# Spreading a norm's row over the partitions: one f32 product per 512 columns becomes two fp32r products of its halves

## The chip, the core and the metric

The kernel runs on one core of a Trainium2 chip. The metric is the device time of one execution in microseconds. Five engines matter: TensorE (PE in the profile; PEld is its weight load), VectorE (DVE), ScalarE (ACT), GpSimd (POOL) and SyncE (SP), which only issues loads and stores. They run side by side and wait for each other by semaphores.

## What is computed

One layer of a decoder step for a prompt of 512 tokens and 32 further tokens (8 sequences of 4). Cut to what matters here:

```
h = rmsnorm(x, g_mix_pre)            # x / sqrt(mean(x*x) + eps) * g, D = 1024
proj = h @ w_in                      # q, k, v, conv input, gelu input, gates
merged = sigmoid(ga) * (attention(q, k, v) @ w_pa) + sigmoid(gr) * (rglru(conv) * gelu(gb) @ w_pr)
x = x + rmsnorm(merged @ w_out, g_mix_post)
x = x + rmsnorm((silu(f @ wg) * (f @ wu)) @ w_down, g_ffn_post)     # f = rmsnorm(x, g_ffn_pre)
```

The change touches the first line: the row `g_mix_pre` (`norm_mix_pre`, 1024 numbers) has to stand in all 128 partitions, as x lies with its tokens on the partitions.

## The kernel before

All arithmetic is in f32 quality. TensorE's fast format for four-byte numbers is fp32r, which keeps fewer bits, so every large product is made of three: each operand is split into a high half (a copy into fp32r) and a low half (the number minus its high half, in fp32r again), and hi*hi, hi*lo and lo*hi are summed in PSUM (`steps`, line 1082; `head_pass`, line 1288). ScalarE makes the high halves of the weights (`hi`, line 1662), VectorE the low ones (`lo`, line 2248); the first low half is GpSimd's (line 946).

The prologue, up to about 20 us, brings x into place. SyncE loads x's token tiles (`x_tok`, four of 128 tokens and one of 32) and the first weights (`w_raw`). ScalarE squares and sums each tile (`x_rms`, line 1684) and takes the root (line 1687). VectorE inverts it (`x_inv`, line 2266) and scales the tile by it and by `g_row` (`x_scale`, line 2271). TensorE transposes the scaled tile (`x_T`, line 1106), ScalarE copies the result from PSUM to `xin_hi` (line 1696), VectorE subtracts to `xin_lo` (`x_lo`, line 2283). Then the first products can run (`head_pass`).

`g_row` comes about like this. VectorE zeroes partitions 0 to 126 of `g_one` (line 2237), and a load puts the norm's row in partition 127 (line 1672). `ones` is a 128x128 tile of ones. TensorE multiplies `ones` with `g_one` in f32, 512 columns at a time (`g_rows`, line 1116), so each partition of the result gets the sum over the partitions, which is the row. VectorE copies each half out of PSUM (`g_copy`, line 2261). Ahead of this, TensorE runs seven transposes of `ident` as fillers (`turn`, line 1113), and more of them between the transposes of x. Behind `g_rows`, TensorE makes the table of position biases (lines 1126 and 1127), which reuses a PSUM bank of the row and so waits for the first copy (`norm_step`), and for the loads of the table (`rel_in`). Behind the first products stand small transposes of parameters (lines 1299 and 1301), which wait for all the loads that GpSimd issues in the beginning (`par_in`).

Each engine works off its own list in the order in which it is written, and a wait holds up all that stands behind it. `norm_step` counts VectorE's steps of the norm; `consts_v` counts its constants; `g_in` is the load of the row. VectorE's order before is copy of g's first half, inverse of tile 0, scaling of its first half, copy of g's second half, scaling of the second half, then tile 1.

Of the kernel before, what the change touches and what calls it, by code (L numbers as in the profile page):

```python
# [23 lines left out]
F32 = mybir.dt.float32  # L24
F32R = mybir.dt.float32r
I32 = mybir.dt.int32
ALU = mybir.AluOpType
ACT = mybir.ActivationFunctionType
AP = bass.AP

P = 128
D = 1024
KD = D // P
# [3 lines left out]
T = SEQ + TS  # L37
# [74 lines left out]
X_ORDER = (0, 1, 2, 3, TT)  # L112
# [18 lines left out]
def program(nc, x_prompt, x_sample, cache_k, cache_v, page_table, state_conv, state_h,  # L131
# [11 lines left out]
    at = [-(-nc.sbuf_base // 64) * 64]  # L143

    def put(name, shape, dt=F32, where=None):
        size = 4 * int(np.prod(shape[1:]))
        size = -(-size // 32) * 32
        if where is None:
            offset, at[0] = at[0], at[0] + size
        else:  # L150
            offset, where[0] = where[0], where[0] + size
        assert offset + size <= nc.sbuf_usable_end, (name, offset + size)
        return nc.alloc_sbuf_tensor_at(name, shape, dt, offset=offset)
# [3 lines left out]
    w_raw, w_hi, w_lo = ring  # L157
    xin_at = at[0]
    xin_hi = put("xin_hi", [P, KD, T], F32R)
    xin_lo = put("xin_lo", [P, KD, T], F32R)  # L160
    ident = put("ident", [P, P])
    ones = put("ones", [P, P])
# [58 lines left out]
    x_sq = put("x_sq", [P, D], where=w)  # L221
    g_row = put("g_row", [P, D], where=w)
    g_one = put("g_one", [P, D], where=w)
    ssum = put("ssum", [P, 8], where=w)
    rstd_x = put("rstd_x", [P, 8], where=w)
    prow = put("prow", [56, P], where=w)
# [157 lines left out]
    with ExitStack() as ctx:  # L384
        def sem(name):
            return ctx.enter_context(nc.semaphore(name))

        ps = ctx.enter_context(nc.psum_tensor("ps", [P, 8, 512], F32))
# [12 lines left out]
        g_in = sem("g_in")  # L401
        g_spread = sem("g_spread")
# [4 lines left out]
        consts_v = sem("consts_v")  # L407
        sq_sum = sem("sq_sum")
        std_x = sem("std_x")
        norm_step = sem("norm_step")  # L410
# [160 lines left out]
        def x_fill(dst, tt, hf, f):  # L571

            if tt < TT:
                return (dst[:, 4 * hf:4 * hf + 4, tt * P:(tt + 1) * P],
                        ps[:, 4 + f % 4, :].rearrange("p (k c) -> p k c", c=P))
            return dst[:, :, SEQ:T], ps[:, 3, 0:KD * TS].rearrange("p (k c) -> p k c", c=TS)
# [495 lines left out]
        def _(e):  # L1072
# [37 lines left out]
            def turn(n):  # L1110

                for _ in range(n):
                    e.transpose(ps[:, 0, 0:P], ident[:, :], ident[:, :])

            def g_rows(hf):
                e.matmul(ps[:, 1 + hf, :], ones[:, :], g_one[:, 512 * hf:512 * hf + 512], start=True, stop=True  # L1116
                         ).then_inc(g_spread, 1)

            turn(7)
            e.wait_ge(consts_v, 6)  # L1120
            e.wait_ge(g_in, 16)
            g_rows(0)
            g_rows(1)
            e.wait_ge(norm_step, 1)
            e.wait_ge(rel_in, 32)
            e.matmul(ps[:, 3, 0:512], rel33[:, :], bktab[:, 0:512], start=True, stop=True)
            e.matmul(ps[:, 1, 0:RELW - 512], rel33[:, :], bktab[:, 512:RELW], start=True,
                     stop=True).then_inc(small_T, 1)
# [528 lines left out]
        def _(e):  # L1657
# [18 lines left out]
            e.dma_start(rel33[0:NB, 0:HEADS], rel_bias).then_inc(rel_in, 16)  # L1676
            e.wait_ge(consts_v, 5)
            e.activation(ycol[:, 0:1], eps_col[:, :], ACT.Sqrt)

            def x_rms(tt):  # L1680

                rows = P if tt < TT else TS
                e.wait_ge(x_in[tt], 16)
                e.activation(x_sq[0:rows, :], x_tok[0:rows, tt, :], ACT.Square,
                             accum_out=ssum[0:rows, tt:tt + 1]).then_inc(sq_sum, 1)
                e.wait_ge(sq_sum, X_ORDER.index(tt) + 1)
                e.activation(rstd_x[0:rows, tt:tt + 1], ssum[0:rows, tt:tt + 1], ACT.Sqrt,
                             bias=eps_col[0:rows, :], scale=1.0 / D).then_inc(std_x, 1)
# [539 lines left out]
        def _(e):  # L2228
# [30 lines left out]
            def g_copy(hf):  # L2259
                e.wait_ge(g_spread, hf + 1)  # L2260
                e.tensor_copy(g_row[:, 512 * hf:512 * hf + 512], ps[:, 1 + hf, :]).then_inc(norm_step, 1)

            def x_inv(tt):
                rows = slice(0, P if tt < TT else TS)
                e.wait_ge(std_x, X_ORDER.index(tt) + 1)
                e.reciprocal(rstd_x[rows, tt:tt + 1], rstd_x[rows, tt:tt + 1]).then_inc(norm_step, 1)

            def x_scale(tt, step, c0=0, c1=D):
                rows = slice(0, P if tt < TT else TS)
                e.wait_ge(norm_step, step)  # L2270
                e.scalar_tensor_tensor(x_tok[rows, tt, c0:c1], x_tok[rows, tt, c0:c1], rstd_x[rows, tt:tt + 1],
                                       g_row[rows, c0:c1], ALU.mult, ALU.mult).then_inc(xs_done, 1)

            def x_norm(tt):
                x_inv(tt)
                x_scale(tt, X_ORDER.index(tt) + 3)

            def x_lo(tt):
                for hf in range(2 if tt < TT else 1):
                    f = X_HALF[tt] + hf  # L2280
                    e.wait_ge(xt_hi, f + 1)
                    dst, src = x_fill(xin_lo, tt, hf, f)
                    e.tensor_tensor(dst, src, x_fill(xin_hi, tt, hf, f)[0].bitcast(F32), ALU.subtract).then_inc(xt_lo, 1)

            g_copy(0)
            x_inv(0)
            x_scale(0, 2, 0, 512)
            g_copy(1)
            x_scale(0, 3, 512, D)
            x_inv(1)  # L2290
            x_scale(1, 4, 0, 512)
            x_scale(1, 4, 512, D)
            x_lo(0)
            x_lo(1)
            x_norm(2)
            e.wait_ge(small_T, 3)
            e.tensor_copy(prm[:, :], ps[:, 2, 0:56]).then_inc(small_c, 1)
            e.tensor_copy(stT[:, :, :], ps[:, 2, 64:64 + P].rearrange("p (f r) -> p f r", f=PAIRS)).then_inc(small_c, 1)
            x_norm(3)
            e.wait_ge(lo_done, 3)  # L2300
            lo(1, 1)
            x_norm(TT)
            x_lo(2)
            x_lo(3)
# [500 lines left out]
            def y_square(m, s):  # L2805
                e.wait_ge(y_free, m + 3)
                if m > 1:
                    e.wait_ge(y_moved, min(m, KD - 3) * 192)
                e.transpose(yz[s][:, :], yg[s][:, :]).then_inc(y_turned, 1)  # L2809
                e.wait_ge(ysq_used, m + 1)  # L2810
                e.tensor_tensor(yacc[:, :], yacc[:, :], ysq[:, :], ALU.add).then_inc(ysq_used, 1)
# [13 lines left out]
            op_sums(0)  # L2825
            op_low(0, 5)
            e.memset(yacc[:, :], 0.0).then_inc(consts_v, 1)
            e.wait_ge(consts_v, 7)
            y_square(0, 0)
            op_low(0, 6)  # L2830
            hs_low(2, 3)
# [75 lines left out]
```

## Time and profile before

| | us |
|---|---|
| median of 3 runs | 761.62 |
| lowest and highest | 760.98, 761.72 |
| the profiled execution | 761.57 |
| its span, first to last instruction | 759.7 |
| TensorE busy in the span | 751.6 (99%) |
| VectorE, ScalarE, GpSimd busy | 519.8, 376.5, 116.4 |

All times in the profile are microseconds from the start of the span. A row of the timeline merges neighbouring instructions of one kind (x4 is four of them): its first number is the start of the first, the second the time from there to the end of the last. Matmuls are pipelined, so the time from one start to the next is what each costs, and the duration of one record is longer than that. A product in f32 has two records for 512 columns.

### The profile page before, as it was taken

The page shows a single profiled execution, that of the slowest core. Times are in us where ns is not written, and L with a number is a line of the kernel's source. Part 1 is how long each engine was busy: PE and PEld are TensorE (multiplying, and loading weights), DVE is VectorE, ACT ScalarE, POOL GpSimd, SP SyncE. Part 2 cuts the span into 40 slices and gives each one's busy share as a digit, 9 for nine tenths or more (in the row PEclk, how much of TensorE's full clock was granted, in tenths as well). Part 3 has the DMA queues.
Part 4 walks back from the last instruction along what each step waited for, and adds up shares of the span by engine and source line. Part 5 has one row for each costly group of instructions (what it writes and reads, how often), then busy time and mean ns, then how long its engine had stood idle before and what let it go on. Part 6 is the DMA issues. An engine that isn't in the chain of part 4 may idle for free.

```text
span 759.7 us, 16105 instructions
## 1 busy us (share of the span) xinstructions
PE 751.6 (99%) x5903; PEld 713.0 (94%) x5903; DVE 519.8 (68%) x823; ACT 376.5 (50%) x670; POOL 116.4 (15%) x228
## 2 busy tenths in 40 slices
PE   9999999999999999999999999999999999999996
PEld 6998899898898999997899999999999999999996
DVE  7547737656675574775469887787777899764644
ACT  7334625534733642344466555455554568454442
POOL 6502112020120110003000000000000000453650
PEclk9999999999999999999999999999999999999998
DMA  9645555545543325517461333223332212424274
GB/s 265 164 112 118 151 118 135 149 113 109 153 115 97 95 65 171 167 56 212 147 190 34 112 110 110 85 81 110 110 110 83 84 50 73 137 75 133 69 227 135
DMA packets 185065, 91.77 MB, mean 121 GB/s; under 512 B 52454, under 2 KB 177850, under 8 KB 185020
## 3 DMA queue, kind: packets, MB, share of 16 engines
q1 hardware_dynamic: 178958, 82.69, 39.8%
q0 software_dynamic: 4880, 8.13, 4.0%
q8 instruction: 28, 0.46, 0.3%
q10 hardware_dynamic: 1182, 0.35, 0.2%
q14 instruction: 17, 0.14, 0.1%
HBM read 82.37 MB, written 6.81 MB: 117 GB/s over the span
## 4 chain that ended last, share of the span: by engine, by line
PE 99%; ACT 0%; DVE 0%; DVEq 0%; issue 0%; POOL 0%; POOLq 0%
PE ps L1082 34%; PE ps L1470 28%; PE ps L1587 7%; PE ps L1365 6%; PE ps L1572 5%; PE ps L1534 4%; PE ps L1438 3%; PE ps L1288 2%; PE ps L1189 1%; PE ps L1203 1%; PE ps L1221 1%; PE ps L1263 1%; PE ps L1174 1%; PE ps L1234 1%; PE ps L1116 0%; PE ps L1373 0%
## 5 line engine op out<-in xcount | busy, mean ns | idle before, releaser
L1082 PE MATMUL ps<-xin_hi,w_hi 128*128 128x272 f32 x544 | 117.1, 296 | 0.0
L1082 PE MATMUL ps<-xin_hi,w_lo 128*128 128x272 f32 x544 | 112.6, 288 | 0.0
L1082 PE MATMUL ps<-xin_lo,w_hi 128*128 128x272 f32 x544 | 112.3, 288 | 0.0
L1082 PEld LDWEIGHTS ps<-xin_hi,w_hi 128*128 128x128 f32 x544 | 84.8, 189 | 8.1 <-issue 7.6
L2248 DVE TENSOR_TENSOR w_lo<-w_raw,w_hi 128x1024 fp32r<-128x1024 f32 (+1 forms) x46 | 55.9, 1216 | 47.6 <-ACT w_hi L1662 46.6
L1082 PEld LDWEIGHTS ps<-xin_lo,w_hi 128*128 128x128 f32 x544 | 85.5, 189 | 0.0
L1082 PEld LDWEIGHTS ps<-xin_hi,w_lo 128*128 128x128 f32 x544 | 85.0, 189 | 0.0
L648 POOL DMA_DIRECT2D ytok<-yz x48 | 33.8, 710 | 307.9 <-DVE yz L2809 307.9
L1662 ACT ACTIVATE w_hi<-w_raw 128x1024 fp32r<-128x1024 f32 (+1 forms) x47 | 49.2, 1050 | 47.9 <-PE ps L1082 44.0
L1470 PE MATMUL ps<-xq_lo,b_hi 128*128 128x272 f32 x160 | 46.7, 292 | 0.0
L1470 PE MATMUL ps<-xq_hi,a_lo 128*128 128x272 f32 x160 | 46.4, 290 | 0.0
L1470 PE MATMUL ps<-xq_lo,a_hi 128*128 128x272 f32 x160 | 46.2, 289 | 0.0
L1470 PE MATMUL ps<-xq_hi,b_hi 128*128 128x272 f32 x160 | 46.2, 289 | 0.0
L1470 PE MATMUL ps<-xq_hi,b_lo 128*128 128x272 f32 x160 | 46.1, 288 | 0.0
L1470 PE MATMUL ps<-xq_hi,a_hi 128*128 128x272 f32 x160 | 46.1, 288 | 0.0
L1470 PE MATMUL ps<-xq_hi,c_hi 128*128 128x272 f32 x160 | 46.1, 288 | 0.0
L1470 PE MATMUL ps<-xq_hi,c_lo 128*128 128x272 f32 x160 | 45.9, 287 | 0.0
L1470 PE MATMUL ps<-xq_lo,c_hi 128*128 128x272 f32 x160 | 45.9, 287 | 0.0
L1985 ACT ACTIVATE a_hi<-g_raw 128x1024 fp32r<-128x1024 f32 x20 | 21.2, 1062 | 21.1 <-PE ps L1470 17.9
L1470 PEld LDWEIGHTS ps<-xq_hi,b_hi 128*128 128x128 f32 x160 | 30.2, 189 | 0.0
L1470 PEld LDWEIGHTS ps<-xq_hi,b_lo 128*128 128x128 f32 x160 | 30.1, 188 | 0.0
L1470 PEld LDWEIGHTS ps<-xq_lo,a_hi 128*128 128x128 f32 x160 | 30.1, 188 | 0.0
(397 smaller groups left out, 2136.6 us busy)
## 6 DMA issues: line engine op xcount, KB each, us to landing
w_raw<-in_w_in_dram SPq DMA_DIRECT2D x68, 256.0 KB, 3.5
g_raw<-in_w_gate_up_dram SPq DMA_DIRECT2D x40, 256.0 KB, 3.8
u_raw<-in_w_gate_up_dram SPq DMA_DIRECT2D x20, 256.0 KB, 3.1
e_raw<-in_w_gate_up_dram SPq DMA_DIRECT2D x20, 256.0 KB, 4.3
raw_p<-in_w_down_dram SPq DMA_DIRECT2D x24, 192.0 KB, 2.5
kc<-in_cache_k_dram SPq DMA_DIRECT2D x64, 64.0 KB
vc<-in_cache_v_dram SPq DMA_DIRECT2D x64, 64.0 KB
raw<-in_w_down_dram SPq DMA_DIRECT2D x12, 320.0 KB, 3.2
```

Of the source, the lines that this page charges most:

```text
L648: e.dma_start(prompt[:, 2 * part:2 * part + 2, d, :], yz[s][rows, c0:c0 + 2 * P]).then_inc(moved, 16)
L1082: mm = e.matmul(ps[:, bank + h, 0:HT], wt[:, kw, :], xt[:, kx, h * HT:h * HT + HT], start=first and wt is wh and xt is xh, stop=last and ( ...
L1288: mm = e.matmul(ps[:, 2 * s + h, 0:cols.stop - cols.start], w[:, k, :], x[:, k, cols], start=first and k == 0, stop=last and k == KD - 1, ...
L1365: mm = e.matmul(ps[:, o_bank(tt) + c, :], xt[:, k, tt * P:tt * P + P], wt[:, c * NHALF:(c + 1) * NHALF], start=k == K_ORDER[0] and xt is x ...
L1438: mm = e.matmul(ps[:, 4 * m + 2 * c + h, 0:HT], wt[:, k, :], xt[:, x, k % KQ, :], start=k == 0 and wt is wh and xt is xq_hi, stop=k == KD ...
L1470: mm = e.matmul(ps[:, bank, 0:HT], wt[:, k0 + k, :], xt[:, x, k, :], start=first and k == 0 and wt is wh and xt is xq_hi, stop=last and k ...
L1534: mm = e.matmul(ps[:, D_BANK[odd] + h, 0:cols.stop - cols.start], wt[:, k, :], x, start=first and k == ks[0] and wt is wh and not lo_x, st ...
L1572: mm = e.matmul(ps[:, bank, 0:HT], wt[:, k, :], xt, start=first and k == 0 and wt is wh and xt is xh, stop=last and k == SK - 1 and wt is ...
L1587: mm = e.matmul(ps[:, banks[h], 0:HT], wt[:, k, :], x, start=firsts[h] and i == 0 and k == 0 and wt is wh and not lo_x, stop=lasts[h] and ...
L1662: e.activation((to or w_hi[s])[:, 0:k, :], w_raw[s][:, 0:k, :], ACT.Copy).then_inc(hi_done, count)
L1985: e.activation(a_hi[:, :, :], g_raw[s][:, :, :], ACT.Copy).then_inc(a_h, 1)
L2248: e.tensor_tensor(wl[:, 0:k, :], w_raw[s][:, 0:k, :], wh[:, 0:k, :].bitcast(F32), ALU.subtract).then_inc(lo_done, count)
```

## The change

It does four things. On VectorE, ahead of everything in the norm, `ones` is copied into an fp32r tile, g_one's first 512 columns are copied into `g_hi`, and the low halves of both parts are made by subtraction into `g_lo`. On ScalarE, after its first root and ahead of the first tile's squares, the other 512 columns are copied into `g_hi`. On TensorE, `g_rows` is two fp32r products (high half, then low half, into one PSUM group) and waits for the halves instead of the raw row; there are eleven filler transposes ahead of it instead of seven; and the bias table waits for a later count of the same semaphore, which is again that of the first copy out of PSUM. On VectorE both copies of `g_row` now come ahead of the inverse of tile 0, and both scalings of a tile wait for one count. The new tiles lie where `xin_lo` will be written later. The other hunks only renumber counts.

```diff
@@ tiles
+    xin_lo_at = at[0]
     xin_lo = put("xin_lo", [P, KD, T], F32R)
...
+    w_lo_ = [xin_lo_at]
+    g_hi = put("g_hi", [P, D], F32R, where=w_lo_)
+    g_lo = put("g_lo", [P, D], F32R, where=w_lo_)
+    ones_r = put("ones_r", [P, P], F32R, where=w_lo_)
@@ TensorE
             def g_rows(hf):
-                e.matmul(ps[:, 1 + hf, :], ones[:, :], g_one[:, 512 * hf:512 * hf + 512], start=True, stop=True
-                         ).then_inc(g_spread, 1)
-
-            turn(7)
-            e.wait_ge(consts_v, 6)
-            e.wait_ge(g_in, 16)
+                half = slice(512 * hf, 512 * hf + 512)
+                e.wait_ge(norm_step, 3 + hf)
+                e.matmul(ps[:, 1 + hf, :], ones_r[:, :], g_hi[:, half], start=True, stop=False)
+                e.matmul(ps[:, 1 + hf, :], ones_r[:, :], g_lo[:, half], start=False, stop=True).then_inc(g_spread, 1)
+
+            turn(11)
             g_rows(0)
             g_rows(1)
-            e.wait_ge(norm_step, 1)
+            e.wait_ge(norm_step, 5)
             e.wait_ge(rel_in, 32)
@@ ScalarE
             e.activation(ycol[:, 0:1], eps_col[:, :], ACT.Sqrt)
+            e.wait_ge(consts_v, 6)
+            e.wait_ge(g_in, 16)
+            e.activation(g_hi[:, 512:D], g_one[:, 512:D], ACT.Copy).then_inc(consts_v, 1)
@@ VectorE
+            e.wait_ge(consts_v, 6)
+            e.tensor_copy(ones_r[:, :], ones[:, :]).then_inc(norm_step, 1)
+            e.wait_ge(g_in, 16)
+            e.tensor_copy(g_hi[:, 0:512], g_one[:, 0:512]).then_inc(norm_step, 1)
+            e.wait_ge(norm_step, 2)
+            e.tensor_tensor(g_lo[:, 0:512], g_one[:, 0:512], g_hi[:, 0:512].bitcast(F32), ALU.subtract).then_inc(norm_step, 1)
+            e.wait_ge(consts_v, 7)
+            e.tensor_tensor(g_lo[:, 512:D], g_one[:, 512:D], g_hi[:, 512:D].bitcast(F32), ALU.subtract).then_inc(norm_step, 1)
             g_copy(0)
+            g_copy(1)
             x_inv(0)
-            x_scale(0, 2, 0, 512)
-            g_copy(1)
-            x_scale(0, 3, 512, D)
+            x_scale(0, 7, 0, 512)
+            x_scale(0, 7, 512, D)
             x_inv(1)
-            x_scale(1, 4, 0, 512)
-            x_scale(1, 4, 512, D)
+            x_scale(1, 8, 0, 512)
+            x_scale(1, 8, 512, D)
```

## Rows read from the trace of the kernel before

**Rows 1.** The page: its span, and the chain that ended last, by engine.
```profile
span 759.7 us, 16105 instructions
...
PE 99%; ACT 0%; DVE 0%; DVEq 0%; issue 0%; POOL 0%; POOLq 0%
```

**Rows 2.** Timeline of TensorE, 1.5 to 12 us: start, time, engine, line, operation, tiles.
```profile
1.53 1.76 PE L1113 MATMUL ps<-ident 128*128 128x128 f32 x7 [1.53 <-POOL ident L928]
...
2.87 0.42 PE L1113 MATMUL ps<-ident 128*128 128x128 f32 x1
...
3.21 3.78 PE L1116 MATMUL ps<-g_one,ones 128*128 128x512 f32 x4
6.86 1.55 PE L1126 MATMUL ps<-bktab,rel 128*128 128x512 f32 x2
...
8.47 0.60 PE L1106 MATMUL ps<-ident,x_tok 128*128 128x128 f32 x4
8.91 0.71 PE L1113 MATMUL ps<-ident 128*128 128x128 f32 x5
...
11.77 1.18 PE L1288 MATMUL ps<-xin_hi,w_hi 128*128 128x256 f32 x8 [0.19 <-ACT xin_hi L1696]
12.88 0.27 PE L1299 MATMUL ps<-ident,prow 56*128 56x56 f32 x1
```

**Rows 3.** Stretch 0 to 13 us: its length, busy times, granted clock, DMA.
```profile
0.00:13.00 13.00, 11.28 (x51) 7.44 (x51) 8.77 (x19) 8.26 (x15) 9.82 (x23) 1.00 0.86 269
```

**Rows 4.** Timeline of VectorE, 2.2 to 14 us.
```profile
2.24 0.91 DVE L2237 MEMSET g_one<- 127x1024 f32 x1 [0.16 <-issue]
5.32 0.69 DVE L2261 COPY g_row<-ps 128x512 f32<-128x512 f32 x1 [2.17 <-PE ps L1116]
6.36 0.16 DVE L2266 RECIPROCAL rstd_x<-rstd_x 128x1 f32<-128x1 f32 x1 [0.35 <-ACT rstd_x L1687]
6.56 0.75 DVE L2271 SCALAR_TENSOR_TENSOR x_tok<-x_tok,rstd_x,g_row 128x512 f32<-128x512 f32 x1
7.22 0.68 DVE L2261 COPY g_row<-ps 128x512 f32<-128x512 f32 x1
7.94 0.75 DVE L2271 SCALAR_TENSOR_TENSOR x_tok<-x_tok,rstd_x,g_row 128x512 f32<-128x512 f32 x1
...
8.80 1.41 DVE L2271 SCALAR_TENSOR_TENSOR x_tok<-x_tok,rstd_x,g_row 128x512 f32<-128x512 f32 x2
```

**Rows 5.** Timeline of ScalarE, 2 to 16.6 us.
```profile
3.64 0.20 ACT L1678 ACTIVATE ycol<-eps_col 128x1 f32<-128x1 f32 x1
4.85 1.06 ACT L1684 ACTIVATE x_sq<-x_tok 128x1024 f32<-128x1024 f32 x1 [1.00 <-DMA x_tok<-in_x_prompt_dram]
...
9.11 0.60 ACT L1696 ACTIVATE xin_hi<-ps 128x512 fp32r<-128x512 f32 x1 [1.09 <-PE ps L1106]
9.60 1.05 ACT L1662 ACTIVATE w_hi<-w_raw 128x1024 fp32r<-128x1024 f32 x1
10.55 1.56 ACT L1696 ACTIVATE xin_hi<-ps 128x512 fp32r<-128x512 f32 x3
```

**Rows 6.** Last parameter load: its issue, its us to landing; TensorE's wait at 16.49.
```profile
6.84 0.50 POOL L937 DMA_DIRECT2D strow<-in_state_h_dram  x1
...
strow<-in_state_h_dram POOLq DMA_DIRECT2D x1, 16.0 KB, 5.9
...
16.49 0.30 PEld L1288 LDWEIGHTS ps<-xin_hi,w_hi 128*128 128x128 f32 x2 [0.23 <-ACT w_hi L1662]
```

**Rows 7.** Chain that ended last, 0 to 40 us: start, us, what.
```profile
13.51 2.11 PE ps L1288 x16
```

**Rows 8.** VectorE's groups by form: busy, mean ns of one, idle before.
```profile
L2458 DVE TENSOR_SCALAR aa<-dd 128x552 f32<-128x552 f32 x4 | 1.8, 450 | 0.1
L2261 DVE COPY g_row<-ps 128x512 f32<-128x512 f32 x2 | 1.4, 688 | 2.2 <-PE ps L1116 2.2
L2369 DVE TENSOR_SCALAR lgt<-lgt,rden 128x128 f32<-128x128 f32 x8 | 2.3, 287 | 0.3
L2234 DVE MEMSET ones<- 128x128 f32 x1 | 0.2, 165 | 0.1
L2283 DVE TENSOR_TENSOR xin_lo<-ps,xin_hi 128x512 fp32r<-128x512 f32 x6 | 3.7, 674 | 0.0
```

More of the change, by code:

```diff
@@ L223, in program @@
     g_one = put("g_one", [P, D], where=w)
+    w_lo_ = [xin_lo_at]
+    g_hi = put("g_hi", [P, D], F32R, where=w_lo_)
+    g_lo = put("g_lo", [P, D], F32R, where=w_lo_)
+    ones_r = put("ones_r", [P, P], F32R, where=w_lo_)
+    assert w_lo_[0] <= xin_lo_at + 4 * KD * T
     ssum = put("ssum", [P, 8], where=w)
@@ L2275, in x_norm @@
                 x_inv(tt)
-                x_scale(tt, X_ORDER.index(tt) + 3)
+                x_scale(tt, X_ORDER.index(tt) + 7)
             def x_lo(tt):
@@ L2827, in _ @@
             e.memset(yacc[:, :], 0.0).then_inc(consts_v, 1)
-            e.wait_ge(consts_v, 7)
+            e.wait_ge(consts_v, 8)
             y_square(0, 0)
```

## The prediction

> **What bounds the kernel now.** I read the page from the top. TensorE is busy nearly all of the 759.7 us span, and the chain of work that ended last is 99% TensorE [rows 1]. The reader is to see that a prologue edit can only matter by when it lets TensorE's unbroken row of products begin: a microsecond that TensorE gains or loses in the first 20 us is carried to the end, and a microsecond of any other engine is worth nothing until TensorE waits for it. The profiled execution took 761.57 us, 1.87 us more than its span; the median of the three runs shown is 761.62 us, so the two agree within 0.05 us. I make the sum against 761.57.
>
> Next I read the prologue on each engine in order of time. On TensorE: seven transposes of `ident` that keep it busy, then the two products that spread the norm's row (four records of 128x512, two to a product), then the bias table, then the first transposes of x at 8.47, with filler transposes between, then the first real product at 11.77 [rows 2]. Two readings of those rows matter.
>
> First, TensorE's clock. The granted clock reads 1.00 for the first 13 us [rows 3], but the spacing of equal records says otherwise: seven `ident` transposes need 1.76 us, with a last one of 0.42 us some 0.21 us from start to start, while five of them at 8.91 need 0.71 us, some 0.11 us each [rows 2]. The four records of 512 columns take 3.78 us and the two of the bias table 1.55 us. So the engine works at the lower level (1.2 GHz) until about 7.8 us, in the middle of the bias table, and at 2.4 GHz after it. It had been at work since 1.53 us, with gaps of about 0.1 us.
>
> Second, who holds TensorE. The products of the norm's row end about 6.8 and the bias table begins at 6.86, so until 8.47 the engine only works off its queue. On VectorE the copy of g's first half waits until 5.32 for its product, and x_tok's first half is scaled from 6.56 to 7.31 [rows 4], over 1.1 us before TensorE takes it up. So before the change it is TensorE, not VectorE, that sets the first transposes. After them ScalarE is late: it idles until 9.11, then runs without a gap the copy to xin_hi, the high half of the first weights (9.60, 1.05 us) and three more copies [rows 5]; the first product waits for one of these, 0.19 us by its row [rows 2]. The transposes of parameters come next, at 12.88. They need every load on GpSimd's list; the last of these is issued at 6.84 and lands 5.9 us later, at 12.74 [rows 6]. That is 0.14 us before its use, and it doesn't move with this change.
>
> **The change part by part.** *Removed:* the two f32 products, 3.78 us of TensorE at the lower clock [rows 2]. By the rows the first needs 2.11 us from its start at 3.21 to the copy at 5.32; two records at 0.85 us (the spacing of the four) are 1.71 of it, and 0.40 is weight load, drain and hand-over.
>
> *Added on TensorE:* four fp32r products of 512 columns. The trace has none of these at the lower clock. Sixteen of 256 columns take 2.11 us at the higher one [rows 7], 0.13 each, so 512 columns at half the clock are 0.53; the floor is half an f32 record, 0.43. I take 0.45 a product: 0.9 a half instead of 1.71. Four more filler transposes (0.85 us) run from 3.0 to 3.9, while the engine would be waiting anyway: free.
>
> *Added on VectorE ahead of the products*, after its memset of g_one that ends 3.15 [rows 4]: a 128x128 copy, between the memset's 0.17 and a TENSOR_SCALAR's 0.29, I take 0.20; the high half of 512 columns, between 0.45 (one source, SBUF to SBUF, 552 columns) and 0.69 (the copy out of PSUM), I take 0.45, as the nearer shape; the low half, 0.68, from the TENSOR_TENSOR of 512 columns into fp32r [rows 8]. With 0.1 for the semaphore increments that stand before them and 0.05 at each of three hand-overs this is 3.15 + 0.1 + 0.20 + 0.45 + 0.68 + 0.15 = 4.73. TensorE begins the products there instead of at 3.21: **1.5 us later**. The second low half (0.68) runs on VectorE until 5.4, under the first pair of products.
>
> The Trainium skill ("VectorE: DVE Perf Modes", perf-mode tier table) says that a single-source fp32 op whose operands lie in SBUF takes two elements a cycle and one that reads PSUM only one. Its cost table would price the high half at 0.33 us, and the sum would start at 4.61. No copy into fp32r on VectorE stands in this trace, so this is untested here.
>
> *Added on ScalarE:* the high half of the other 512 columns, not over 0.6 us (the copies to xin_hi have that shape). ScalarE is free at 3.84 and its next work begins at 4.85, when x_tok has landed [rows 5]. It ends by 4.5: nothing. Without that cover it would cost what sticks out, and the first square sum with it. What is queued behind its two new waits is that same square sum; both waits are over by 3.2.
>
> *Moved on VectorE:* both copies of g_row now stand ahead of the reciprocal and the scaling. Pair one ends at 4.73 + 0.9 + 0.4 = 6.03, the copy at 6.72. Pair two ends 0.9 later, 6.93, the copy 7.62. The reciprocal with its hand-overs takes until 7.85, x_tok's first half until 8.60 (it was 7.31), the second, started 0.67 later as in rows 4 (7.94 to 8.61), until 9.27 (8.69), and tile 1 until 10.8 (10.21). Queued behind them are the low halves of xin, which wait for ScalarE's copies, from 11.2 on but for the first: they keep their time.
>
> *What TensorE makes of it.* The bias table now waits for the first copy, 6.72, and TensorE is free at about 6.6; the load of that table stands in the same wait as before. It begins near 6.86 as before and ends at 8.47 as before. So the 1.6 us that the products save are eaten by their later start and by the wait for the copy. The first transposes of x then wait for VectorE: 8.60 + 0.05 = 8.65 instead of 8.47, **+0.18 us**. The later ones don't wait: with the fillers between, the second half of tile 0 is asked for at 9.6 (ready 9.27), tile 1's halves near 10.5 (10.05) and 10.95 (10.8). ScalarE's row of copies moves by the same 0.18, the first product goes from 11.77 to 11.95 and the transposes at 12.88 to 13.06. ScalarE's row decides again at 16.49, where TensorE waits 0.23 us for the second w_hi [rows 6], and that moves by 0.18 too. No later stage is touched.
>
> *Bounds.* With the low ends (0.17, 0.45, 0.43 a product) the delay is about 0. With the high ends (0.29, 0.69, 0.53) it is some 0.33 before the products and 0.32 for two pairs more: +0.8. A gain is capped too. If all of it came earlier, the transposes at 12.88 could move by 0.14 at most, as their last load lands at 12.74, and the wait at 16.49 could give back 0.2: not over 0.35 us.
>
> **The rivals.** *B, the higher clock comes later: slower than before.* Before, TensorE works from 1.53 to 7.8 almost without a gap and then runs at 2.4 GHz. After, it idles from about 4.1 to 4.7 and again from 6.6 to 6.86. If the rise is put off past the bias table, that table and all transposes double: TensorE reaches the first transposes of x at about 9.17 and finishes them at 10.0, so ScalarE begins at 10.26 instead of 9.11, +1.15. For each further group at the lower clock 0.4 to 0.5 is added: with a rise near 11.2, tile 1's first half is some 1.6 late; with one past 13.6, 2.8. I price it at +1.6: 763.2. It passes 0.2% (1.5 us, about what a measurement of this kernel can tell from no change) if the rise comes later than about 11 us. For it: the fillers were there before, one after the other, and the new gap is the only long one after 1.53. Against it: the work from 4.7 to 7.8 has only that second gap of 0.26 us, and the first stretch, 1.5 to 3.2, was the same kind of filler. The Trainium skill ("TensorE: Matmul & The Clock Gate", "Why this matters for your kernels") speaks against this change: it says that the clock starts low and goes up only after sustained work, and advises to leave no gaps before it has.
>
> *C, two fp32r products of the halves are no cheaper than one f32 product: the change doesn't do what it says.* Pair one then ends at 4.73 + 2.11 = 6.84, pair two near 8.3, and the first scaling ends about 9.9: x is transposed 1.5 late, 763.1. Against it stands 0.13 us for 256 columns of fp32r at the higher clock, where the f32 record of 512 takes 0.43 and two go to a product.
>
> *D, a small gain.* If the higher clock comes earlier in the new kernel, or the first copy is done sooner than I think, the cap above holds: -0.3, 761.3. For it speaks only that the four products leave TensorE free earlier.
>
> **How the numbers follow.** A, the forecast: +0.2 on 761.57 gives 761.8, chance 0.72; B 0.17; C 0.04; D 0.07. A's own range is 761.1 to 762.5, of which 0.7 is what the three runs before spread by (760.98 to 761.72) and the rest the bounds. The range has to take in B's and C's nearer half: 761.1 to 763.2. Faster by over 0.2% would need 1.5 us, more than four times the cap; I leave 0.03 for something the trace doesn't show. Slower by over 0.2% is the part of B and C beyond 763.1 and a remainder: 0.12. The rest, 0.85, is no difference.
>
> **What would show it.** In the changed trace: the first product of the norm's row at 4.7 on TensorE, each pair 0.9 long; the bias table at 6.9 with its second record at the higher clock; x_tok's first scaling ending at 8.6; the first transposes of x at 8.65, ScalarE's first copy to xin_hi at 9.3, the first product at 11.95. Spacings of 0.21 us among the transposes after 8.5 would be B. Pairs of 1.7 us would be C. The first product before 11.7, with the parameters still at 12.88, would be D with its gain absorbed. The prediction is wrong if another wait appears after 13 us, or if the new copy on ScalarE pushes the first square sum past 4.85.

## The result and the profile after

The changed kernel took 763.12 us (median of 11 runs, 762.11 to 764.19), the kernel before 761.28 us (760.95 to 762.21) beside it. The ratio is 1.0019, 95% interval 1.0011 to 1.0027: a loss of 0.2%, small, but the interval doesn't reach 1. The second comparison gave 1.0024 (1.0015 to 1.0033). The profiled execution took 762.69 us, 1.12 more than that of before; its span is 760.9.

The timeline of TensorE in the changed kernel, as rows 2:

```profile
1.54 2.61 PE L1119 MATMUL ps<-ident 128*128 128x128 f32 x11 [1.54 <-POOL ident L934]
4.68 0.80 PE L1124 MATMUL ps<-g_hi,ones_r 128*128 128x512 f32 x1 [0.54 <-DVE g_lo L2299]
5.28 0.63 PE L1125 MATMUL ps<-g_lo,ones_r 128*128 128x512 f32 x1
5.70 0.63 PE L1124 MATMUL ps<-g_hi,ones_r 128*128 128x512 f32 x1
6.13 0.63 PE L1125 MATMUL ps<-g_lo,ones_r 128*128 128x512 f32 x1
6.69 1.85 PE L1132 MATMUL ps<-bktab,rel 128*128 128x512 f32 x2
8.38 0.39 PE L1133 MATMUL ps<-bktab,rel 128*128 128x128 f32 x2
8.60 0.60 PE L1112 MATMUL ps<-ident,x_tok 128*128 128x128 f32 x4
...
11.90 1.18 PE L1294 MATMUL ps<-xin_hi,w_hi 128*128 128x256 f32 x8 [0.19 <-ACT xin_hi L1705]
13.08 0.26 PE L1305 MATMUL ps<-ident,prow 56*128 56x56 f32 x1
```

From the second on, the four fp32r products start 0.43 us apart (0.60 from the first to the second), where the four f32 records of before were 0.85 apart. The four together take 2.08 us (4.68 to 6.76) instead of 3.78, so 1.70 us less, but they begin at 4.68 instead of 3.21 [rows 2]. The bias table starts at 6.69 instead of 6.86. It then takes 1.85 us instead of 1.55, because the higher clock comes near 8.2 and not near 7.8 (the second record of the table starts at 7.70 and the next product at 8.38; at the lower clock that takes 0.85 us, at the higher 0.43). The granted clock of the profile reads 1.00 for the first 13 us here too and doesn't show this. So the first transposes of x begin 0.13 us late, and so does the first product, at 11.90.

VectorE in the same stretch, as rows 4, with the new operations:

```profile
3.34 0.23 DVE L2295 CAST ones_r<-ones 128x128 fp32r<-128x128 f32 x1 [0.18 <-DVE g_one L2246]
3.48 0.42 DVE L2297 CAST g_hi<-g_one 128x512 fp32r<-128x512 f32 x1
3.93 0.69 DVE L2299 TENSOR_TENSOR g_lo<-g_one,g_hi 128x512 fp32r<-128x512 f32 x1
4.54 0.68 DVE L2301 TENSOR_TENSOR g_lo<-g_one,g_hi 128x512 fp32r<-128x512 f32 x1
5.94 0.69 DVE L2270 COPY g_row<-ps 128x512 f32<-128x512 f32 x1 [0.71 <-PE ps L1125]
6.79 0.69 DVE L2270 COPY g_row<-ps 128x512 f32<-128x512 f32 x1 [0.16 <-PE ps L1125]
7.40 0.15 DVE L2275 RECIPROCAL rstd_x<-rstd_x 128x1 f32<-128x1 f32 x1
7.59 1.42 DVE L2280 SCALAR_TENSOR_TENSOR x_tok<-x_tok,rstd_x,g_row 128x512 f32<-128x512 f32 x2
```

The first scaling ends at 8.34. That is later than before (7.31) and still ahead of TensorE, which is free only at 8.60. ScalarE's new copy is a row of its own, under the cover named:

```profile
3.75 0.61 ACT L1687 ACTIVATE g_hi<-g_one 128x512 fp32r<-128x512 f32 x1
4.55 1.06 ACT L1693 ACTIVATE x_sq<-x_tok 128x1024 f32<-128x1024 f32 x1 [0.19 <-DMA x_tok<-in_x_prompt_dram]
```

**Where the profiled execution's 1.1 us went.** I set the start of each matmul of the two traces side by side. The difference grows in steps and is level between them: 0.13 us at the first product, 0.12 to 0.20 until 27 us, 0.39 from 28 us, and 1.13 from 670 us to the end. The second step is a wait of TensorE's weight load that the kernel before doesn't have; the third is one late load of the down weights. The rows of TensorE's weight load near 28 us and of its products near 670 us:

```profile
27.88 0.30 PEld L1088 LDWEIGHTS ps<-xin_hi,w_hi 128*128 128x128 f32 x2 [0.22 <-DVE w_lo L2264]
...
670.58 0.52 PE L1593 MATMUL ps<-hid_hi,op_hi 128*128 128x272 f32 x2 [0.50 <-DVE op_lo L2787]
```

Behind the second, in the chain of waits, stands a load of raw_p (two rows of that chain):

```profile
661.02 4.83 DMA raw_p<-in_w_down_dram
665.85 0.02 issue
```

The median load of raw_p lands after 2.6 us in this kernel and 2.5 in the kernel before; this one took 4.8.

### The profile page after: what moved, and what is told of

It reads as the page before. It is cut to its first block, busy times and chain, and to the rows that moved or that the text cites. A ratio compares the mean times of both kernels' runs of the same rounds, so it can differ in the third digit from the quotient of the medians.

```text
span 760.9 us, 16118 instructions
## 1 busy us (share of the span) xinstructions
PE 751.7 (99%) x5907; PEld 714.0 (94%) x5907; DVE 521.5 (69%) x827; ACT 377.2 (50%) x671; POOL 116.5 (15%) x228
## 4 chain that ended last, share of the span: by engine, by line
PE 96%; ACT 1%; DVE 1%; DMA 1%; issue 1%; DVEq 0%; ACTq 0%
PE ps L1088 34%; PE ps L1476 28%; PE ps L1593 6%; PE ps L1371 6%; PE ps L1578 5%; PE ps L1540 4%; PE ps L1444 3%; PE ps L1195 1%; PE ps L1209 1%; PE ps L1227 1%; PE ps L1294 1%; PE ps L1269 1%; DMA raw_p<-in_w_down_dram 1%; PE ps L1180 1%; PE ps L1240 1%
## 5 line engine op out<-in xcount | busy, mean ns | idle before, releaser
L1593 PE MATMUL ps<-hid_hi,op_hi 128*128 128x272 f32 x144 | 29.9, 289 | 0.5 <-DVE op_lo L2787 0.5
```

The lines of the kernel that those rows point to most:

```text
L1593: mm = e.matmul(ps[:, banks[h], 0:HT], wt[:, k, :], x, start=firsts[h] and i == 0 and k == 0 and wt is wh and not lo_x, stop=lasts[h] and ...
```

## The experiments

**First set: the same kernels again, and the number of fillers.** `b_again` and `a_again` are the two kernels unchanged. `a_turn7` and `b_turn11` change one number:

```diff
# a_turn7, from the changed kernel
-            turn(11)
+            turn(7)
# b_turn11, from the kernel before
-            turn(7)
+            turn(11)
```

> The kernel before once more, against itself: ratio 1.000, within 0.1%. Its use is a second trace. Theory S (steady causes): its trace repeats the first one, first products at 11.77 us, the product at 27.6 us without a wait, no wait of TensorE on a low half of the down weights between 640 and 755 us. Theory R (random late loads): in some traces of this kernel too TensorE waits for a load of the down weights by half a microsecond or more.

Measured: 761.42 us, ratio 0.9996 (0.9987 to 1.0004). First product at 11.64, no wait near 28 us and none on the down weights.

> The changed kernel once more: ratio 1.0019 again if the loss is steady. Theory S: its trace has the same three steps behind the kernel before, 0.13 us at the first product, some 0.25 at 27.9 us where VectorE's small op overlaps GpSimd's copies, and 0.7 us near 670 us where a load of the down weights lands late; sum 1.1 us. Theory R: the first two are there (0.4 us), the third is in this trace or not, at a place of its own. Theory B (the clock): the first transposes of x are spaced 0.21 us instead of 0.11 in this execution and the loss is in the prologue, 1 to 2 us.

Measured: 764.02 us, ratio 1.0024 (1.0015 to 1.0033). The profiled execution took 764.45 us, and it is theory B's. TensorE, then its weight load near 30 us:

```profile
6.69 2.08 PE L1132 MATMUL ps<-bktab,rel 128*128 128x512 f32 x2
8.55 0.64 PE L1133 MATMUL ps<-bktab,rel 128*128 128x128 f32 x2
8.98 1.06 PE L1112 MATMUL ps<-ident,x_tok 128*128 128x128 f32 x4
9.84 1.18 PE L1119 MATMUL ps<-ident 128*128 128x128 f32 x5
10.85 0.60 PE L1112 MATMUL ps<-ident,x_tok 128*128 128x128 f32 x4
...
13.10 1.07 PE L1294 MATMUL ps<-xin_hi,w_hi 128*128 128x256 f32 x7
```

```profile
30.35 0.30 PEld L1088 LDWEIGHTS ps<-xin_hi,w_hi 128*128 128x128 f32 x2 [1.48 <-DVE w_lo L2264]
```

Four transposes of x take 1.06 us at 8.98 and 0.60 at 10.85: the lower level (1.2 GHz) until about 10.7 us, then 2.4 GHz. The first product comes 1.33 us later than in the kernel before, and near 28 us the loss is doubled: 1.4 us before that point, 2.9 behind it. There is no late load in this trace. So the steps of the first trace are not steady: here the loss is the clock's late rise and a second wait that is longer than in the first trace.

The second wait is explained by VectorE and GpSimd in this trace. VectorE has a row of some twenty tiny operations on `sp` and `prm`, each waiting for the one before, and behind it the low half of the next weights. GpSimd copies the biases:

```profile
25.19 3.58 DVE L2347 SCALAR_TENSOR_TENSOR sp<-sp,sp 128x4 f32<-128x4 f32 x9
28.80 0.17 DVE L2349 SCALAR_TENSOR_TENSOR sp<-sp,sp 128x4 f32<-128x4 f32 x1
29.00 0.17 DVE L2351 TENSOR_SCALAR prm<-sp 128x4 f32<-128x4 f32 x1
29.08 2.45 DVE L2264 TENSOR_TENSOR w_lo<-w_own,w_hi 128x1024 fp32r<-128x1024 f32 x2
```

```profile
25.45 2.47 POOL L966 COPY bias_s<-bias_rev 128x256 f32<-128x256 f32 x4 [2.99 <-DMA bias_rev<-dist_shift]
27.87 1.17 POOL L968 COPY bias_s<-bias_rev 128x16 f32<-128x16 f32 x8
```

In the kernel before the nine operations take 1.74 us and the row is over at 26.10, just as GpSimd starts:

```profile
23.96 1.74 DVE L2330 SCALAR_TENSOR_TENSOR sp<-sp,sp 128x4 f32<-128x4 f32 x9
...
25.93 0.17 DVE L2334 TENSOR_SCALAR prm<-sp 128x4 f32<-128x4 f32 x1
...
26.02 3.54 POOL L960 COPY bias_s<-bias_rev 128x256 f32<-128x256 f32 x4 [3.00 <-DMA bias_rev<-dist_shift]
```

VectorE's row hangs on the prologue. GpSimd's start hangs on loads and moves by itself: where nothing else holds it, it lies between 25.07 and 26.54 in the twelve traces, in no order with the prologue. Whether the two meet depends on both. Where they do, a tiny operation ends only when the copy beside it does: in this trace the four beside the copies of 128x256 take 0.54 to 0.58 us each and the three beside the short copies of 128x16 take 0.24, against 0.16 for one that runs alone. The Trainium skill ("SBUF — State Buffer", "Who interferes with whom") says that GpSimd and VectorE share one pair of ports, which whoever comes first holds for its whole instruction; the trace agrees.

> The changed kernel with 7 filler transposes instead of 11, so TensorE idles from 3.1 to 4.7 us. TensorE's list is then eight instructions shorter, as long as that of the kernel before. If the late load near 670 us comes from where instruction fetches fall (these run on the same 16 DMA engines), it goes away and the ratio falls to 1.0005. If theory B holds, the longer gap puts the rise of the clock off further: first product at 13 us or later and a ratio of 1.002 to 1.004. If neither, 1.0019 as for the changed kernel.

Measured: 763.86 us, ratio 1.0023 (1.0013 to 1.0032). With TensorE's list as short as that of the kernel before, a late load (0.4 us near 718 us) was there all the same, though not near 670 us. So the loss doesn't go away with the length of the list, which speaks against the idea of the instruction fetches as its cause. The ratio is in theory B's range, the trace only in part: the clock rose near 9.4, the first product came at 12.60 and not past 13, and TensorE waited 1.4 us for VectorE at 29.8. The longer pause cost no more than the shorter one.

> The kernel before with 11 filler transposes instead of 7: the norm's row starts 0.85 us later on TensorE (4.05) and everything of the prologue that TensorE bounds moves by up to 0.8: first product at 12.5, in all +0.8 us, ratio 1.001. If the place of the instruction fetches matters, the late load near 670 us appears here too and the ratio is 1.002. If the clock rises by a count of work and not at a set time, it rises at the same moment, 7.8 us.

Measured: 762.29 us, ratio 1.0003 (0.9995 to 1.0012). The interval still holds the ratio that was expected, but the trace went the other way. TensorE's row of f32 products, begun at 3.94, took 2.69 us instead of 3.78:

```profile
3.94 2.69 PE L1116 MATMUL ps<-g_one,ones 128*128 128x512 f32 x4
6.71 1.10 PE L1126 MATMUL ps<-bktab,rel 128*128 128x512 f32 x2
...
11.16 1.25 PE L1288 MATMUL ps<-xin_hi,w_hi 128*128 128x256 f32 x8
12.82 0.27 PE L1299 MATMUL ps<-ident,prow 56*128 56x56 f32 x1 [0.42 <-DMA strow<-in_state_h_dram]
```

The clock rose near 5.6 us. The first product came 0.6 us sooner than before, and all of it was lost again in front of the parameters' load, at 12.82: the cap that the prediction put on a gain. A late load near 670 us is in this trace too (0.3 us), as the idea of the instruction fetches would have it, but the ratio isn't the 1.002 that went with it. The rise came after less time and fewer products than in the kernel before, so it is tied to no fixed moment and no fixed amount of products. That the four more fillers brought it forward isn't shown by this one trace: with nothing changed the rise moves by over 2 us from one execution of the changed kernel to the next. TensorE also waited 0.65 us for VectorE at 27.7, though the prologue was early: GpSimd's copies began at 25.27 here, and met VectorE's row all the same.

**Second set: the two causes taken away, one by one and together.** `a_pool` and `b_pool` make GpSimd wait, before its copies, until VectorE's tiny operations are done. `a_turn14` fills the pause. `a_turn14_pool` does both.

```diff
# a_pool (changed kernel) and b_pool (kernel before)
             e.wait_ge(bias_moved, 16 * (DEC_T + 1 + PAIRS))
+            e.wait_ge(small_c, 4)
# a_turn14, from the changed kernel
-            turn(11)
+            turn(14)
```

> The changed kernel; GpSimd waits, ahead of its four copies to bias_s (line 966), for the end of VectorE's row of tiny operations on prm and sp, so the two no longer run side by side. Theory P (the prologue's delay is doubled because those tiny operations then run beside GpSimd's copies and take up to 0.6 us each, and TensorE waits for the low half behind them): no wait of TensorE near 27.6 to 30 us; the loss is the prologue's alone, 0.1 to 1.4 us with the clock; ratio 1.0008 to 1.0012 instead of 1.0022. Theory K (the wait near 28 us comes from something else): it stays, 0.2 to 1.5 us, ratio 1.002.

Measured: 762.21 us, ratio 1.0011 (1.0000 to 1.0021), half of the loss. The clock rose near 8.8, the first product came at 12.23, 0.46 late. Behind it the difference to the kernel before stayed at 0.49 us until the end: nothing was doubled. In this trace VectorE's nine operations took 1.74 us, ahead of GpSimd:

```profile
24.32 1.74 DVE L2348 SCALAR_TENSOR_TENSOR sp<-sp,sp 128x4 f32<-128x4 f32 x9
```

```profile
26.61 3.28 POOL L967 COPY bias_s<-bias_rev 128x256 f32<-128x256 f32 x4 [3.87 <-DVE prm L2352]
```

> The kernel before with the same wait on GpSimd. In its two traces the tiny operations end at the moment in which GpSimd's copies begin or before it, so theory P expects nothing: 1.0000 within 0.1%. If bias_s, now later by under 1 us, were needed in time, TensorE would show a new wait before 60 us and the ratio would rise by 0.05 to 0.1%.

Measured: 761.75 us, ratio 1.0006 (0.9996 to 1.0015); no new wait of TensorE in its trace. No difference that can be told, as expected, though the interval is wide.

> The changed kernel with 14 filler transposes: TensorE works until 4.6 us and the row's products begin at 4.7 as they did, so the gap before them is 0.1 us instead of 0.5 to 0.7. Theory B (the gap puts the clock's rise off in some executions): the rise comes by 8.3 us in all of them, first product at 11.9, ratio 1.0003 to 1.0008. If the gap doesn't matter: the rise still comes at 8 to 10.7 us from one execution to the next, ratio 1.002.

Measured: 762.19 us, ratio 1.0008 (0.9999 to 1.0016). TensorE:

```profile
1.54 3.25 PE L1119 MATMUL ps<-ident 128*128 128x128 f32 x14 [1.54 <-POOL ident L934]
4.68 0.80 PE L1124 MATMUL ps<-g_hi,ones_r 128*128 128x512 f32 x1
...
6.69 1.12 PE L1132 MATMUL ps<-bktab,rel 128*128 128x512 f32 x2
7.65 0.38 PE L1133 MATMUL ps<-bktab,rel 128*128 128x128 f32 x2
8.34 0.66 PE L1112 MATMUL ps<-ident,x_tok 128*128 128x128 f32 x4 [0.30 <-DVE x_tok L2280]
...
11.69 0.95 PE L1294 MATMUL ps<-xin_hi,w_hi 128*128 128x256 f32 x6 [0.19 <-ACT xin_hi L1705]
```

Three more fillers, and the bias table takes 1.12 us instead of 1.85 or 2.08: the rise came before 6.7. Now TensorE waits for VectorE, as the prediction had it for the changed kernel, at 8.34 instead of 8.65. This trace has the wait near 28 us (0.6) and a late load (0.3); they make up its 762.43 us. The wait near 28 us doesn't come from a late prologue here: VectorE's nine operations start at 23.78, sooner than in the kernel before, but GpSimd's copies start at 25.53.

> Both edits together. Theories B and P: nothing of the loss is left but 0.1 us at the first product; ratio 1.0000 to 1.0004. If only P holds: as with the wait on GpSimd alone.

Measured: 761.74 us, ratio 1.0003 (0.9995 to 1.0012). First product at 11.77, to the hundredth that of the kernel before, and 0.22 us behind it at the end. The loss can't be told from nothing any more. There is no gain either: with the cheaper products and without a pause, this kernel isn't faster than the one before.

**Third set: the products by themselves, and the fillers in front.**

```diff
# a_f32, from the changed kernel
-                e.matmul(ps[:, 1 + hf, :], ones_r[:, :], g_hi[:, half], start=True, stop=False)
-                e.matmul(ps[:, 1 + hf, :], ones_r[:, :], g_lo[:, half], start=False, stop=True).then_inc(g_spread, 1)
+                e.matmul(ps[:, 1 + hf, :], ones[:, :], g_one[:, half], start=True, stop=True).then_inc(g_spread, 1)
# b_turn0, from the kernel before
-            turn(7)
+            turn(0)
```

> The changed kernel, with all its waits, splits and fillers, but with the row spread by the old f32 product of 512 columns from ones and g_one instead of two fp32r ones. It shows what the cheaper products are worth by themselves, and whether the gap alone or the shorter work behind it puts off the clock. By the rows: a product of 1.7 us at the lower clock instead of 0.86; first copy at 6.8 instead of 5.94, second at 8.0 to 8.5, x transposed from 9.5 on, first product near 12.9, then the doubling near 28 us; ratio 1.003. If the gap ahead of the products is what puts off the rise, it comes at 8 us or later here too. If it is the little work of the fp32r products, it comes by 7.8.

Measured: 764.71 us (764.65 to 764.80), ratio 1.0040 (1.0026 to 1.0054).

```profile
4.68 3.78 PE L1124 MATMUL ps<-g_one,ones 128*128 128x512 f32 x4 [0.53 <-DVE g_lo L2298]
8.26 1.91 PE L1131 MATMUL ps<-bktab,rel 128*128 128x512 f32 x2
9.96 0.47 PE L1132 MATMUL ps<-bktab,rel 128*128 128x128 f32 x2
...
13.57 0.59 PE L1293 MATMUL ps<-xin_hi,w_hi 128*128 128x256 f32 x3 [0.19 <-ACT xin_hi L1704]
```

The clock rose near 10.1, though TensorE was busy with f32 products from 4.68 on. So a late rise doesn't need the short fp32r products; the pause ahead of them is there in both. This is one trace, and the ratio is 1.004 where 1.003 was expected. The bias table starts at 8.26 instead of 6.69, so the cheaper products by themselves are worth about 1.6 us there, and 0.5 to 1.7 us of the first product's start (13.57 against 11.90 to 13.10).

> The kernel before without the seven filler transposes in front: TensorE idles until 3.2 us and then works on as before. If the work before 3.2 us has no part in the rise: the same times, rise by 7.8, ratio 1.000. If it has: the rise comes later in some executions, as in the changed kernel with its gap, first product at up to 13 us, ratio up to 1.002.

Measured: 762.08 us, ratio 1.0009 (1.0000 to 1.0019). In its trace TensorE begins at 3.26, the clock rises near 8.75, the first product comes at 12.28 and TensorE waits 1.5 us for VectorE near 28: 763.64 us. In this trace the old kernel has the loss of the new one, with no fp32r product in it; its ten runs together have about half of it, and their interval reaches to no loss.

**Two more looks.**

> A third trace of the changed kernel, for how its executions differ. Expected: the higher clock somewhere between 8 and 10.6 us; the wait of TensorE near 28 us the longer the later the rise (0.2 us at a first product of 11.90, 1.5 at 13.10 so far); a late load between 640 and 755 us in it or not.

Measured: 762.75 us; rise near 9.2, first product 12.42, wait 0.5 us near 28, no late load. The wait was shorter than the rise would have it: GpSimd's start moves too.

> A third trace of the kernel before: the higher clock between 7.3 and 7.9 us, first product at 11.5 to 11.8, no wait near 28 us; a late load between 640 and 755 us in it or not.

Measured: 762.65 us, one of the longer executions of this kernel. The clock rose near 6.8, but the loads were late: the bias table waited 0.17 us for its own, the first product came at 12.13 behind ScalarE, and TensorE waited 0.54 us for the parameters' load until 13.86. A wait of 0.5 near 28 followed. No late load of the down weights.

**All traces together.** The rise is read from the spacing of equal records (0.85 or 0.43 us for 512 columns of f32, 0.21 or 0.11 for a transpose) and is good to about 0.1 us. The column "row, copies" has the time at which VectorE's row of tiny operations would end undisturbed (2.14 us after the nine begin, as in the kernel before), and the time at which GpSimd's copies begin.

| trace | TensorE before the rise | rise | first product | row, copies | wait near 28 | us |
|---|---|---|---|---|---|---|
| before | at work since 1.53 | 7.8 | 11.77 | 26.10, 26.02 | 0 | 761.57 |
| `b_again` | the same | 7.7 | 11.64 | 25.89, 26.54 | 0 | 761.43 |
| `b_pool` | the same | 7.4 | 11.49 | 25.78, 26.50 | 0 | 761.26 |
| `b_look2` | the same | 6.8 | 12.13 | 26.37, 26.19 | 0.5 | 762.65 |
| `b_turn11` | the same | 5.6 | 11.16 | 25.65, 25.27 | 0.7 | 762.29 |
| `a_turn14` | the same | by 6.7 | 11.69 | 25.92, 25.53 | 0.6 | 762.43 |
| `a_turn14_pool` | the same | 6.9 | 11.77 | 26.00, 26.15 | 0 | 761.75 |
| `b_turn0` | idle until 3.26 | 8.75 | 12.28 | 26.51, 25.07 | 1.5 | 763.64 |
| after | pause before 4.68 | 8.2 | 11.90 | 26.21, 26.01 | 0.2 | 762.69 |
| `a_look2` | the same | 9.2 | 12.42 | 26.74, 26.25 | 0.5 | 762.75 |
| `a_pool` | the same | 8.8 | 12.23 | 26.46, 26.61 | 0 | 762.05 |
| `a_again` | the same | 10.7 | 13.10 | 27.33, 25.45 | 1.5 | 764.45 |
| `a_f32` | the same | 10.1 | 13.57 | 27.81, 25.77 | 1.5 | 764.80 |
| `a_turn7` | longer pause before 4.68 | 9.4 | 12.60 | 26.83, 26.14 | 1.4 | 764.40 |

Seven traces in which TensorE works from 1.53 on have the rise at 5.6 to 7.8; seven with a pause, or a start at 3.26, have it at 8.2 to 10.7. The two groups don't overlap, though 7.8 and 8.2 lie close. The wait near 28 us follows the column before it: none while the row would end before the copies begin or within 0.1 us behind it, 0.2 to 0.7 us where it would end 0.2 to 0.5 us behind it, 1.4 to 1.5 us from 0.7 us on.

## Why the prediction was right and where it was wrong

The measured 763.12 us lies just inside the range (761.1 to 763.2), and a difference of under 0.2% was given 0.85. But the likeliest case, A at 761.8, was not what happened; the time is that of rival B, which had 0.17 and was priced at 763.2. That it meets B's price is in part luck. B put all of its 1.6 us into the prologue. The three traces of the changed kernel have 0.13, 0.65 and 1.33 us there; the rest is the wait near 28 us (0.2, 0.5 and 1.5), which the prediction didn't have, and in one of them a late load (0.7).

**VectorE's new operations and the start of the products: right.** Forecast 4.73, measured 4.68. The casts took 0.23 and 0.42, the low half 0.69, a product 0.43 at the lower clock (forecast 0.45), but 0.60 from the first to the second. The rule that the Trainium skill gives for single-source fp32 operations ("VectorE: DVE Perf Modes", perf-mode tier table) holds for the cast into fp32r too: 0.42 us, against 0.69 for the copy of as many elements out of PSUM. The 0.33 us of that page's cost table is too low for it; the page says itself that this row under-predicts a single operation.

**ScalarE's copy costs nothing: right.** 0.61 us, over at 4.36; the square sum behind it waited for its load until 4.55.

**Which engine the first transposes wait for: wrong.** The forecast was VectorE, +0.18. I had VectorE's first scaling end at 8.60; it ended at 8.34: the second copy was over at 7.48 instead of 7.62, and the reciprocal ran right behind it, so that the scaling began at 7.59 instead of 7.85. TensorE began the bias table at 6.69 instead of the 6.86 that I had. With the rise at 7.8 it would have been free at about 8.4 (an estimate: 8.47 less half of the 0.17 us, as those 0.17 us are worked at the lower clock), when VectorE's half was ready too. It was free at 8.60, because the rise was 0.4 us late. The size of the step (+0.13) came out near for another reason. Only with the pause filled (`a_turn14`) does TensorE wait for VectorE, and then the first product isn't late.

**The clock at 7.8: the step that failed.** The sum took the rise from the one trace of before and held it fixed. It varies from one execution to the next, and the pause that the change brings in moves it: 8.2, 9.2, 10.7 in three traces of the changed kernel, against 6.8 to 7.8 in three of the kernel before and in `b_pool`, whose prologue is the same. With the pause filled it was back at 6.7 and 6.9. I had named the pause and the mechanism in rival B and argued it down because the later work was nearly unbroken and the first stretch was mere fillers. Both arguments fell, each by one trace: in `b_turn0`, without the fillers in front, the rise came at 8.75, and in `a_f32`, with full work from 4.68 on, at 10.1. B's price for the prologue (+1.15 and more) fits: +1.33 with a rise at 10.7.

**"No later stage is touched": wrong.** A late prologue pushes VectorE's row of tiny operations under GpSimd's copies near 26 us, and TensorE then waits another 0.2 to 1.5 us for the low half behind them. The prologue isn't the only way into that wait: the copies' own start moves too, and with an early start `b_turn11` and `a_turn14` had 0.7 and 0.6 us of it after an early first product. That the row ended in the kernel before in the very moment in which GpSimd began (26.10 and 26.02) was to be read in its trace; I had stopped at 20 us. `a_pool` takes this part away and halves the loss, from 1.0024 to 1.0011; `a_turn14` takes the pause away and leaves 1.0008; both together leave 1.0003. The intervals of the single steps overlap, so the halves are rough; that the two together end the loss stands on 1.0003 (up to 1.0012) against 1.0024 (from 1.0015); against the first comparison, 1.0019 (from 1.0011), the intervals overlap a little.

**The cap on a gain: right.** `b_turn11` had its first product 0.6 us sooner, and the parameters' load took it back at 12.82.

**Left open.** What sets the moment of the rise within one kernel, and why GpSimd's loads land earlier or later, is not shown. A late load of down weights cost TensorE 0.3 to 0.7 us in four of the fourteen traces: after, `a_turn7`, `a_turn14`, `b_turn11`. It isn't in the other two traces of the changed kernel and in none of the four of the kernel before with seven fillers (`b_pool` among them). Three of the four lie near 670 us and in kernels with eleven or more fillers, but five other traces with as many have none. So whether the length of TensorE's list or the change makes it likelier is open. It is 0.7 of the 1.1 us in the first pair of traces, and a study that had stopped at these would have named the wrong cause.

## What to carry to other kernels

A cheaper product gains nothing where the engine then waits for the next thing: even with the pause filled and the second wait taken away, this one gave 1.0003. It can lose if what prepares it opens a pause while TensorE's clock is still low: fill the start without a gap, and count a clock's rise as something that moves with the edit and from one execution to the next. Follow each delay to the next place where two engines meet by chance of timing, for a row of tiny dependent operations that just clears another engine's copies can double it. One pair of traces shows where one execution lost its time, not where the kernel loses it: take several before naming a cause.

## What the runs showed of the hardware

The same kernel saw TensorE go from the lower level to the higher at 8.2, 9.2 and 10.7 us in three traces, with the work before 8.2 us alike to 0.01 us. Fillers that are only transposes of `ident` have their part in it: three more of them, which fill the pause, and the rise came at 6.7 and 6.9 in two traces instead of 8.2 to 10.7 in four (the three and `a_pool`). The single traces point the same way: 8.75 without the seven in front of the kernel before, 5.6 with eleven. The Trainium skill ("TensorE: Matmul & The Clock Gate", "Why this matters for your kernels") advises to leave no gaps before the clock is up, and the traces agree.

Tiny operations of VectorE (128x4) that run beside GpSimd's copies of 128x256 take 0.6 us instead of 0.16. In a row in which each waits for the one before, this is paid again for each: nine of them, seven beside copies, took 3.58 us instead of 1.74.
